# Modulation sums on four column groups, and all first loads of the modulation ahead of the weights

## The reference

```
def adaln_modulation(c, w, b):
    mod = jax.nn.silu(c) @ w + b            # w is 1024 x 6144
    return [m[:, None, :] for m in jnp.split(mod, N_MOD, axis=-1)]
...
    for layer in range(DEPTH):              # DEPTH = 2
        shift_m, scale_m, gate_m, shift_f, scale_f, gate_f = adaln_modulation(c, *ada[layer])
        h = rmsnorm(x, pre_m) * (1.0 + scale_m) + shift_m
        x = x + gate_m * rmsnorm(mixers[layer](h), post_m)
        h = rmsnorm(x, pre_f) * (1.0 + scale_f) + shift_f
        x = x + gate_f * rmsnorm(swiglu(h, *ffns[layer]), post_f)
```

## Time and profile before

| what | us |
|---|---|
| median of 3 runs (lowest, highest) | 1943.56 (1940.8, 1944.72) |
| the profiled execution | 1943.31 |
| its span in the trace | 1941.1 |
| PE busy | 1867.3 (96%) |
| DVE busy | 1442.8 (74%) |
| ACT busy | 991.3 (51%) |
| POOL busy | 257.8 (13%) |

### The profile page before, as it was taken

The page is one execution under the profiler, slowest core; times in us unless marked ns, Lnnn a source line. Parts: engine busy times, 40 slices in busy tenths (PEclk is TensorE's granted clock), DMA queues, the critical chain, the costliest instruction groups (busy, mean ns, idle before and its releaser), DMA issues.

```text
span 1941.1 us, 31807 instructions
## 1 busy us (share of the span) xinstructions
PE 1867.3 (96%) x12460; PEld 1688.7 (87%) x12460; DVE 1442.8 (74%) x2603; ACT 991.3 (51%) x1428; POOL 257.8 (13%) x118
## 2 busy tenths in 40 slices
PE   6999999999998999999999899999999999999998
PEld 5987799999987788889988899999988888888887
DVE  5898875568769775567666579888878887777776
ACT  5655544455455644465555555666643334444444
POOL 0001044430001244420000373000000000000000
PEclk9999999999999999999999999999999999999999
DMA  8763476756574365555344344677766765464452
GB/s 318 241 217 135 149 265 249 259 205 232 181 256 165 123 229 179 191 178 206 143 159 168 120 163 163 200 215 216 217 240 249 281 239 217 179 249 180 186 205 109
DMA packets 94548, 391.89 MB, mean 202 GB/s; under 512 B 7680, under 2 KB 41776, under 8 KB 56000
## 3 DMA queue, kind: packets, MB, share of 16 engines
q1 hardware_dynamic: 94112, 389.59, 56.7%
q10 hardware_dynamic: 288, 0.26, 0.0%
HBM read 371.74 MB, written 15.73 MB: 200 GB/s over the span
## 4 chain that ended last, share of the span: by engine, by line
PE 75%; DVE 14%; ACT 2%; issue 2%; DMA 1%; POOL 0%; DVEq 0%; ACTq 0%
PE ps L615 9%; PE acc L599 9%; PE acc L601 9%; PE acc L600 9%; PE ps L616 5%; PE ps L603 5%; PE ps L604 5%; PE ps L605 5%; PE acc L603 3%; PE acc L604 3%; PE acc L605 3%; DVE wlo L1512 2%; DVE arena L1541 2%; PE acc L1467 1%; PE ps L1467 1%
## 5 line engine op out<-in xcount | busy, mean ns | idle before, releaser
L2603 ACT ACTIVATE whi<-raw 128x1024 fp32r<-128x1024 f32 x553 | 584.2, 1059 | 427.4 <-PE acc L601 206.1
L1512 DVE TENSOR_TENSOR wlo<-raw,whi 128x1024 fp32r<-128x1024 f32 x457 | 556.3, 1224 | 276.0 <-ACT whi L2603 275.6
L1512 POOL TENSOR_TENSOR wlo<-raw,whi 128x1024 fp32r<-128x1024 f32 x96 | 240.0, 2503 | 605.5 <-ACT whi L2603 605.2
L599 PE MATMUL acc<-whi,chi 128*128 128x512 f32 x744 | 293.9, 395 | 4.3 <-DVE wlo L1512 1.9
L601 PE MATMUL acc<-wlo,chi 128*128 128x512 f32 x744 | 291.2, 391 | 0.0
L600 PE MATMUL acc<-whi,clo 128*128 128x512 f32 x744 | 290.5, 390 | 0.0
L615 PE MATMUL ps<-hpair,whi 128*128 128x512 f32 x784 | 278.8, 397 | 1.4 <-POOL wlo L1512 1.4
L603 PE MATMUL ps<-hpair,whi 128*128 128x256 f32 x912 | 262.8, 288 | 4.3 <-DVE wlo L1512 3.1
L604 PE MATMUL ps<-hpair,whi 128*128 128x256 f32 x912 | 258.6, 284 | 0.0
L605 PE MATMUL ps<-hpair,wlo 128*128 128x256 f32 x912 | 258.5, 283 | 0.0
L616 PE MATMUL ps<-hpair,wlo 128*128 128x256 f32 x784 | 219.8, 280 | 0.0
(11 more groups left out here) (509 smaller groups left out, 3101.4 us busy)
## 6 DMA issues: line engine op xcount, KB each, us to landing
raw<-in_peer_down SPq DMA_DIRECT2D x64, 1024.0 KB, 4.9
raw<-in_peer_up SPq DMA_DIRECT2D x64, 1024.0 KB, 5.0
arena<-in_ada SPq DMA_DIRECT2D x80, 512.0 KB, 4.7
raw<-in_w_gate SPq DMA_DIRECT2D x22, 1024.0 KB, 4.8
raw<-in_w_up SPq DMA_DIRECT2D x22, 1024.0 KB, 4.9
raw<-in_w_down SPq DMA_DIRECT2D x22, 1024.0 KB, 4.8
arena<-spill SPq DMA_DIRECT2D x14, 1024.0 KB, 6.8
spill<-hT_t SPq DMA_DIRECT2D x22, 448.0 KB, 6.3
```

The source lines that it names most:

```text
L599: e.matmul(out, xh, hi, start=start, stop=False, skip_group_check=True)
L1512: e.tensor_tensor(out=lo, in0=w, in1=hi.bitcast(F32), op=ALU.subtract).then_inc(*X(("lo", j)))
L2603: e.activation(hi, w, ACT.Copy, scale=1.0).then_inc(*self.A(("hi", j)))
```

## The change

The sum over partitions of a background group is turned round. The four products now have 32 columns of ones as the stationary operand and 128 columns of `ada_acc` as the moving one, and write to partitions 0 to 31, 32 to 63, 64 to 95 and 96 to 127 of one bank: four column groups of the array. DVE copies the 128 x 128 result to `ada_rows` in SBUF. At the next piece PE multiplies it with a constant of four columns (`fours`, ones at partitions 0, 32, 64 and 96), which turns it to 128 x 4, and DVE adds the bias. So a group takes two banks instead of one, and its end is spread over two pieces. In the prologue, SP issues all eight modulation transfers ahead of `w_low` 0; the cuts of `w_low` 0 follow them on ACT and DVE, its second block goes to POOL (which also puts the low passes of its second half ahead of the last four low parts of the input in `pe_first`), block 2 is cut on ACT behind the normed input, and the first product takes bank 4 instead of bank 0. The sums of the prologue itself are as before.

```
@@ constants and tiles
-      ("inv", 1), ("sgn", 1), ("j16", 16), ("ind", 8), ("pick", 16), ("groups", 30)]
+      ("inv", 1), ("sgn", 1), ("j16", 16), ("ind", 8), ("pick", 16), ("groups", 30), ("fours", 4)]
-FIRST = (("w_gate0", 0, 1), ("w_gqk", 0, 1), ("w_gate1", 0, 1), ("w_mqk", 0, 1))
+FIRST = (("w_low", 0, 1), ("w_gate0", 0, 1), ("w_gqk", 0, 1), ("w_gate1", 0, 1), ("w_mqk", 0, 1))
+        self.ada_rows = self.arena[:, NARENA - 128:NARENA]
+    c["fours"] = i[:, None] == 32 * np.arange(4)[None, :]
@@ PE
+    def pe_ada_turn(self, e):
+        if self.ada_due["P"]:
+            layer, g = self.ada_due["P"].pop()
+            e.wait_ge(*self.at("out", "ada_rows", layer, g))
+            ps = self.banks.take(e, "ada", layer, g)
+            e.matmul(ps[:, 0:4], self.m.ada_rows, self.m.kc("fours"), start=True, stop=True, skip_group_check=True).then_inc(
+                *self.P(("full", "ada", layer, g)))
     def pe_ada(self, e, sooner=0):
+        self.pe_ada_turn(e)
...
-            ps = self.banks.take(e, "ada", layer, g)
+            ps = self.banks.take(e, "ada_rows", layer, g)
             for j in range(4):
-                i = e.matmul(ps[:, j * 128:(j + 1) * 128], self.m.ada_acc[:, j * 128:(j + 1) * 128], self.m.ones, start=True,
-                             stop=True, skip_group_check=True)
-            i.then_inc(*self.P(("full", "ada", layer, g)))
+                i = e.matmul(ps[32 * j:32 * j + 32, 0:128], self.m.ones[:, 0:32], self.m.ada_acc[:, j * 128:(j + 1) * 128],
+                             start=True, stop=True, skip_group_check=True)
+            i.then_inc(*self.P(("full", "ada_rows", layer, g)))
+            self.ada_due["P"].append((layer, g))
     def pe_ada_until(self, e, layer, part):
         while self.ada_no["P"] <= ADA.index((layer, 2 * part + 1, 3)) + 1:
             self.pe_ada(e)
+        self.pe_ada_turn(e)
     def pe_proj0(self, e):
+        self.banks.turn = 4
@@ DVE
+    def ve_ada_turn(self, e):
+        if self.ada_due["V"]:
+            layer, g = self.ada_due["V"].pop()
+            c0 = 48 * layer + 4 * g
+            e.wait_ge(*self.at("full", "ada", layer, g))
+            e.tensor_tensor(out=m.mod_t[:, c0:c0 + 4], in0=self.banks.tile("ada", layer, g)[:, 0:4],
+                            in1=m.pv(f"ada_b{layer}", 4 * g, 4), op=ALU.add).then_inc(*self.V(("out", "ada", layer, g)))
     def ve_ada(self, e):
+        self.ve_ada_turn(e)
...
-            e.wait_ge(*self.at("full", "ada", layer, g))
-            e.tensor_tensor(out=m.mod_t[:, c0:c0 + 4], in0=ps[:, :].rearrange("p (a n) -> p a n", a=4)[:, :, 0],
-                            in1=m.pv(f"ada_b{layer}", 4 * g, 4), op=ALU.add).then_inc(*V(("out", "ada", layer, g)))
+            e.wait_ge(*self.at("full", "ada_rows", layer, g))
+            e.tensor_copy(m.ada_rows, self.banks.tile("ada_rows", layer, g)[:, 0:128]).then_inc(
+                *V(("out", "ada_rows", layer, g)))
+            self.ada_due["V"].append((layer, g))
     def ve_ada_until(self, e, layer, part):
...
+        self.ve_ada_turn(e)
@@ DVE, prologue
-                if k == 1 and g == 3:
-                    self.cut_lo(e, V, 0)
-        self.cut_lo(e, V, 1)
         self.ve_mod(e, 3)
...
         e.wait_ge(*self.at("end", "pro", "V"))
+        self.cut_lo(e, V, 0)
         self.ve_normed(e, "mix0", m.coef, m.mod(0, 0), m.hT, m.hH, m.hL)
@@ ACT, prologue
-                    if (g, k) == (3, 6):
-                        self.cut_hi(e, 1)
...
-        self.cut_hi(e, 2)
+        self.cut_hi(e, 1)
...
         self.se_normed(e, "mix0", m.coef, m.mod(0, 0), m.hT, m.hH)
+        self.cut_hi(e, 2)
@@ SP, prologue
-                if (g, h) == (3, 1):
-                    e.dma_start(self.W.slab(0)[0], D["w_low"][0]).then_inc(self.W.slots[0], 16)
                 e.dma_start(m.ada4[:, g, 2 * h:2 * h + 2, :], ...
+        e.dma_start(self.W.slab(0)[0], D["w_low"][0]).then_inc(self.W.slots[0], 16)
```

More of the change, by code:

```diff
@@ L566, in begin @@
         self.banks.begin()
-        self.ada_no = {"P": 0, "V": 0}
+        self.ada_no, self.ada_due = {"P": 0, "V": 0}, {"P": [], "V": []}
         self.squares_made, self.junk_written = 0, [None, None]
@@ L1516, in ve_cuts @@
         self.cut_lo(e, self.V, self.W.last(name, last, width) + 2)
+    def ve_ada_turn(self, e):
+        m = self.m
+        if self.ada_due["V"]:
[4 more added lines that the diff above has]
+                            in1=m.pv(f"ada_b{layer}", 4 * g, 4), op=ALU.add).then_inc(*self.V(("out", "ada", layer, g)))
     def ve_ada(self, e):
         m, V = self.m, self.V
+        self.ve_ada_turn(e)
         s = self.ada_no["V"]
@@ L1526, in ve_ada @@
             layer, g, _ = ADA[s - 1]
-            c0 = 48 * layer + 4 * g
-            ps = self.banks.tile("ada", layer, g)
-            e.wait_ge(*self.at("full", "ada", layer, g))
-            e.tensor_tensor(out=m.mod_t[:, c0:c0 + 4], in0=ps[:, :].rearrange("p (a n) -> p a n", a=4)[:, :, 0],
-                            in1=m.pv(f"ada_b{layer}", 4 * g, 4), op=ALU.add).then_inc(*V(("out", "ada", layer, g)))
+            e.wait_ge(*self.at("full", "ada_rows", layer, g))
+            e.tensor_copy(m.ada_rows, self.banks.tile("ada_rows", layer, g)[:, 0:128]).then_inc(
+                *V(("out", "ada_rows", layer, g)))
+            self.ada_due["V"].append((layer, g))
         if s < len(ADA):
```

## The result

The kernel after takes 1948.8 us (median of 8 runs, 1945.8 to 1950.86), the kernel before beside it 1940.89 us (8 runs). The ratio is 1.0035, 95% interval 1.0024 to 1.0045: 6.8 us slower (4.7 to 8.7). I had forecast 1942.5, that is 0.8 us less than the profiled execution of before, no measurable change. Two executions beside these experiments lasted far longer than all others, one of before 2062 us and one of pro_bank0 4726 us; I can't explain them, and the ratios leave them out. The profiled execution of after took 1950.33 us with a span of 1948.5.

What follows compares the result with a forecast made beforehand. PE was taken as the bound in most places, DVE in some. Terms -0.4 - 2.3 - 0.1 + 0.6 + 0.6 + 0.8 = -0.8 us from 1943.31 gave 1942.5 us; range 1937.5 to 1946.5.

Steps and rivals of the forecast that it cites:

- rival 2: At the turns: PE stands with its queue, +3.2, and one idle stretch halves the clock, +1.7; 1947.4 us, chance 0.12.
- Rival 3: In the background sums: the four column groups run one after another, +5.9; 1948.4 us, chance 0.03.
- -0.4 forecast: Prologue: PE starts 4.3 us sooner, but DVE's first background piece only 0.4 us sooner; -0.4 us, bounds -4.3 and +1.7.
- the gains come at 36.05: Prologue: last modulation transfer lands at 32.1, plus 3.95 us from landing to gains; gains at 36.05 instead of 38.61.
- POOL's 2.5 us cut: Prologue: block 1 cut on POOL from 36.7 to 39.2, not needed by PE before 42, so hidden; uncovered, up to 2.5.
- the group at 546: Three pieces in a row near 546: the group saves 0.4 but PE waits at once for DVE's copy; -0.1 us.
- The first output product: First output product, near 184 us: the turn waits for DVE's copy behind a softmax, partly on the path; +0.6 us.
- Ahead of the gate rows: Ahead of the gate rows, both layers: copy comes behind DVE's gate, so gate rows start 0.4 later; +0.8 us together.
- PE's 1.1 us: `w_z`: PE's new 1.1 us wait for the copy is hidden by a 1.86 us wait at 145.49; DVE's 0.2 isn't.
- 12 x -0.19 = -2.3: Twelve groups where PE is the bound: sum saves 0.41, turn costs 0.22, net -0.19 each; -2.3 us.
- Rivals 1: Prologue: PE's whole 4.3 us earlier start lives on instead of 0.4, `w_xbc` starting at 61; 1938.6 us, chance 0.18.
- 4 (1940.5): PE-bound groups: column groups save more, the turn costing 0.05, 12 x -0.17 = -2.0; 1940.5 us, chance 0.15.

Runs made afterwards that it cites:

- pro_bank0: pro_only without its other first bank: the first product of `w_low` goes into bank 0 again; 1944.54 us, ratio 1.001 to before.
- groups_only: The kernel before with the background groups' edits alone (four column groups, copy, turn) and the prologue of before; 1948.31 us, ratio 1.0031.
- pro_fix: pro_only with DVE cutting block 0 while awaiting the last sum, POOL cutting behind the gains, ACT cutting block 2 ahead of the tiles; 1942.49 us, ratio 1.0000.
- pool_later: The kernel after, where POOL waits with its cut of block 1 until DVE has cut block 0; 1947.98 us, ratio 1.003 to before.
- wait_only: The kernel before, where PE waits ahead of the next piece until DVE has taken up the sum, no work added; 1945.53 us, ratio 1.0011.
- late_turn: The kernel after with turns two pieces behind the sum instead of one, except ahead of the gate rows and at the last group; 1946.92 us, ratio 1.0026.
- groups_best: groups_only with the turn two pieces behind the sum and the sum of before in the two groups ahead of the gate rows; 1945.47 us, ratio 1.0011.
- mended: groups_best with the prologue of pro_fix; 1945.63 us, ratio 1.0016 to before.
- pro_only: The kernel before with the prologue edits alone, background groups as before; 1944.82 us, ratio 1.0008.
- narrow4: The kernel before with 4 moving columns instead of 128 in each of a group's four products, no column groups, copy or turn; 1942.69 us, ratio 1.0002.
- narrow_old: narrow4 with 128 moving columns again in the two groups between 545 and 570 us; 1942.47 us, ratio 1.0002 to before.
- mended_old: mended with the sum of before in two more groups, those between 545 and 570 us; 1944.42 us, ratio 1.0008 to before.
- fill_turns: groups_only, where PE runs 2 to 7 products of ones before it waits at the eight turns where it stood; 1948.02 us, ratio 1.0035 to before.
- cols_only: The kernel before with sums on four column groups, but neither DVE's copy nor the turn (modulation values differ); 1942.14 us, ratio 1.0007.

## Why the prediction was wrong

The size of a group's sum and turn was right. What failed is the prologue, the count of the groups with PE as the bound, two waits that I overlooked, and the granted clock, which stood in a bound and in rival 2 (+1.7 each) but at nothing in the sum. Rival 2 (1947.4, given 0.12) came nearest by its mechanism, new waits and more half clock, though not in the places that it names. Rival 3's 1948.4 is nearer by number, and that is luck: its groups one after another are not in the trace, where a sum takes 0.35 us to the next product.

**The prologue: -0.4 forecast, +1.6 (-0.8 to 3.9) and +3.3 measured on two bases.** Two steps failed. First, "from landing to gains was 3.95 us, so the gains come at 36.05" took both numbers from one profile in which the slab had come late: ACT's cut of it began 4.04 us behind the transfer before it (32.10 - 28.06), where six of the other nine executions with this prologue have 2.5. The last transfer was taken up at 30.74, not 32.1, and the gains were 5.6 us behind it, not 3.95, since the products of two transfers now lie in a row on PE, 32 instructions in 3.74 us from 31.47. Against a prologue without that delay the gains come 0.9 us sooner, not 2.56 (from the seventh transfer's scaling to the gains 9.0 us in groups_only, 36.85 - 27.85, and 8.1 in after, 36.34 - 28.20). The moved cuts cost the 2 us that I had worked out, and there was only 0.9 to pay them with. Second, POOL's 2.5 us cut was called hidden by looking at who waits for its result. It was not hidden from DVE, whose gains it stretched by 1.25 us in after. pro_fix takes away the moved cuts and POOL's overlap at once, and the edits cost nothing then (-1.7 to 1.7). How the cost divides is open: pool_later, which takes away POOL's overlap alone, gives back 1 us, within its interval.

**The waits at the turns: +2.1 (0.6 to 3.9) for a wait alone.** I had counted the group at 546 as "0.1" and overlooked those at 449 and 569, where two or three pieces also come in a row: 0.69 us each from step to step, and 0.49 and 0.45 more in wait_only's d. The other places came out near the forecast. The first output product was given 0.6 (the sum printed there, 0.9 + 0.2 - 0.4, is 0.7), and d rises by 0.7. Ahead of the gate rows the turn stands 1.73 us, but PE stood 0.53 there in before: from the sum to the gate rows it was 1.69 us and is 2.13, the 0.4 forecast, and only 0.2 to 0.3 of it is left in d behind them. In `w_z` PE's 1.1 us was hidden and DVE's own 0.2 a group was not, as forecast; what I missed is the 0.46 us that came back by way of POOL. The group in `w_xbc` cost nothing.

**The groups with PE as the bound: 12 x -0.19 = -2.3 forecast.** A sum saves 0.35 where I had 0.41, and the turn costs the 0.22 forecast. But over 66 to 545 us, with nine of the twelve groups, the columns give 2.6 where I had 0.41 x 9 = 3.7. At 249 us PE waits for DVE's cut right behind the sum, before and after, so nothing is saved there, and the turn and the copy add 0.2 in after; what the group near 462 saves is lost in a wait at 477.

**The clock: no term.** Read from after's trace, the places of the group edits up to 545 us add up to about 2 us, an estimate: 0.9 in `w_z`, 0.7 at 186, 0.2 at the first gate rows, 0.2 at 249, -0.6 over five groups and 0.4 from 440 to 545; behind these only the second gate rows add 0.2 that can be told from the clock. groups_only measured 6.0 (1.9 to 10.1). Its mean granted clock over all executions is 0.9932, against 0.9957 of before beside it. It is 0.9934 in late_turn, 0.9942 in groups_best against 0.9951, and 0.9941 in mended against 0.9958 (without the execution of 2062 us); but 0.9951 in wait_only against 0.9952, and 0.9961 in pro_fix against 0.9958. At the 0.8 to 1.5 us per 0.001 that the executions of before show within one session, this goes with 1 to 4 us, which is the size of what is left, and it makes part of groups_best's 3.9 us as well. So a lower clock comes with the group edits and not with the wait alone. What brings it is open. One thing goes with it: between 540 and 640 us all five profiled kernels with the sum of before (before, wait_only, pro_only, pro_fix, pro_bank0) have 3.4 us at half clock, and all fourteen with another sum, narrow4 and narrow_old among them, have 6.8 to 27.3, each in one profile. But putting the old sum back in the two groups there did not undo it, and narrow4 and narrow_old are no slower than before. With every located wait mended, mended_old is 1.5 us above before (interval -0.2 to 3.3).

Right were the 0.4 us between sum and next product, the two steps into and out of the four groups, and the places of the waits near 111, 184, 216 and 644. Rivals 1 (w_xbc at 61), 3 (groups in series) and 4 (1940.5) are out. That more half clock follows from PE's standing, part of rival 2, is not borne out by wait_only and fill_turns.

## What to carry to other kernels

A transposition that needs another engine in the middle makes the first engine wait with its whole queue; price it in each place by when the other engine gets there and by how long the first one stood there before, and look at every place where pieces come in a row. Before a saving is multiplied by a number of places, look in each for the wait right behind it. Ask of a moved cut not only who needs its result but whom its engine locks out meanwhile. And take a stage's baseline from several executions: 1.5 us of one late transfer was more than all that the prologue edit could win.

## What the runs showed of the hardware

- A DVE instruction of 0.17 us with two SBUF operands lasted 1.31, 1.42 and 2.32 us where POOL's two-input cut of 2.34 us overlapped it, and ended with it each time. A DVE multiply-add of 0.75 us lasted 1.21 us beside a POOL instruction of 1.91 us that ended 0.66 us after it began.
- In before and narrow4, products of 128 x 128 in f32 come as two instructions 0.11 us apart, with 128 moving columns as with 4, while each weight load takes 186 to 192 ns. A load of 32 columns takes 106 to 110 ns. Two instructions with 4 columns whose load has come early are 0.14 us from the next product, and the product behind them is 0.08 to 0.09 us longer on its way to its own successor.
- The same kernel runs at different mean clocks from one execution to the next: cols_only took 1937.95 to 1943.41 us at 0.995 to 0.997 seven times and 1948.47 to 1952.59 us at 0.989 to 0.991 five times, and the one profile of the longer kind has one stretch of 23.8 us at half clock.
